# Attention's last four feature blocks are turned in mid-group, and the output projection waits for the rest only later

## What is computed

```python
x = x + 0.5 * _swiglu(_rmsnorm(x, ffn1_norm[l]), ...)
h = _rmsnorm(x, mix_norm[l])
...
x = x + jnp.concatenate([out_a, out_b, out_c], axis=-1) @ w_out[l]
x = x + 0.5 * _swiglu(_rmsnorm(x, ffn2_norm[l]), ...)
```

## Time and profile before

| | us |
|---|---|
| median of 3 runs | 3964.32 |
| lowest and highest | 3961.46 and 3968.23 |
| the profiled execution, its own time | 3960.14 |
| its span | 3958.5 |

### The profile page before, as it was taken

The page is one execution under the profiler, slowest core; times in us unless marked ns, Lnnn a source line. Parts: engine busy times, 40 slices in busy tenths (PEclk is TensorE's granted clock), DMA queues, the critical chain, the costliest instruction groups (busy, mean ns, idle before and its releaser), DMA issues. The chain is left out here.

```text
span 3958.5 us, 52357 instructions
## 1 busy us (share of the span) xinstructions
PE 3764.8 (95%) x18864; PEld 3120.0 (79%) x18864; DVE 2414.1 (61%) x4293; ACT 1457.2 (37%) x2499; POOL 132.3 (3%) x288
## 2 busy tenths in 40 slices
PE   8999989999899998999989999899999889898999
PEld 6888777888688877788868888788888658687887
DVE  6767674766667668476764355455555674645555
ACT  4223363222422245422245456322222454533322
POOL 0000030000000002100000000000000000000000
PEclk9999999999999999999999999999999999999999
DMA  6443303443544331244321110122121110003332
GB/s 240 134 137 95 104 22 122 134 137 107 188 133 138 101 101 43 88 143 131 118 78 48 59 45 21 58 65 64 58 64 58 46 36 1 27 16 97 96 95 74
DMA packets 100285, 348.72 MB, mean 88 GB/s; under 512 B 10963, under 2 KB 14547, under 8 KB 99336
## 3 DMA queue, kind: packets, MB, share of 16 engines
q1 hardware_dynamic: 73732, 264.97, 21.3%
q0 software_dynamic: 16960, 62.92, 4.9%
q10 hardware_dynamic: 9412, 18.41, 1.3%
HBM read 344.11 MB, written 12.63 MB: 90 GB/s over the span
## 5 line engine op out<-in xcount | busy, mean ns | idle before, releaser
L227 PE MATMUL ps<-h_hi,w_hi 128*128 128x512 f32 (+1 forms) x2824 | 1092.6, 387 | 78.5 <-DVE h_lo L469 34.9
L228 PE MATMUL ps<-h_lo,w_hi 128*128 128x512 f32 (+1 forms) x2824 | 1081.1, 383 | 0.0
L229 PE MATMUL ps<-h_hi,w_lo 128*128 128x512 f32 (+1 forms) x2824 | 1080.0, 382 | 0.0
L227 PEld LDWEIGHTS ps<-h_hi,w_hi 128*128 128x128 f32 x2824 | 537.3, 190 | 195.8 <-issue 41.6
L191 ACT ACTIVATE w_hi<-w_first_raw 128x1024 fp32r<-128x1024 f32 x302 | 319.4, 1059 | 972.5 <-PE ps L229 968.6
L228 PEld LDWEIGHTS ps<-h_lo,w_hi 128*128 128x128 f32 x2824 | 537.3, 190 | 103.1 <-issue 3.4
L229 PEld LDWEIGHTS ps<-h_hi,w_lo 128*128 128x128 f32 x2824 | 536.4, 190 | 103.1
L205 DVE TENSOR_TENSOR w_lo<-w_first_raw,w_hi 128x1024 fp32r<-128x1024 f32 x310 | 379.3, 1224 | 359.8 <-ACT w_hi L191 359.3
L227 PE MATMUL ps<-a_hi,w_hi 128*128 128x512 f32 x1472 | 549.9, 374 | 10.0 <-DVE x L750 6.8
L228 PE MATMUL ps<-a_lo,w_hi 128*128 128x512 f32 x1472 | 546.8, 371 | 0.0
L229 PE MATMUL ps<-a_hi,w_lo 128*128 128x512 f32 x1472 | 545.8, 371 | 0.0
(11 more groups left out here) (295 smaller groups left out, 4662.5 us busy)
## 6 DMA issues: line engine op xcount, KB each, us to landing
w_first_raw<-in_w_first SPq DMA_DIRECT2D x214, 512.0 KB, 3.6
w_raw<-in_w_first SPq DMA_DIRECT2D x104, 512.0 KB, 3.6
shared<-in_w_ada POOLq DMA_DIRECT2D x96, 512.0 KB, 4.4
w_first_raw<-in_w_mlp SPq DMA_DIRECT2D x64, 512.0 KB, 3.6
w_raw<-in_w_mlp SPq DMA_DIRECT2D x64, 512.0 KB, 3.6
bias_rows<-bias_line ACTq DMA_DIRECT2D x2, 5120.0 KB
w_first_raw<-in_w_even SPq DMA_DIRECT2D x16, 512.0 KB, 3.5
near_stage<-in_near POOLq DMA_DIRECT2D x32, 256.0 KB, 2.9
```

Source lines behind the costliest of these rows:

```text
L227: pe.matmul(out, lhs[0], rhs[0], start=start, stop=False)
L228: pe.matmul(out, lhs[0], rhs[1], start=False, stop=False)
L229: return pe.matmul(out, lhs[1], rhs[0], start=False, stop=stop)
```

## The change

Three things. The first turn step of the last group (only where a query block is two groups) moves from after the last unit to unit 8g + 4, into the other bank of the pair; its blocks 0 to 3 are the output of the group before. The projection's wait is cut in parts: in the first stack it waits at its first tile for all turn steps but the last, and for the last at its third tile; in the odd layer it waits only at the third tile; in the even layer the first tile does the 512 tokens first, after the wait for all but the last step, then waits for the last step and does the context. The wait for `out_done` goes.

```diff
@@ Project.tensor
-                o_ready(pe)
+
+                def part(g, p, q, s):
+                    n, stream = self.n0 + 4 * g + p, self.streams[s]
+                    for f in range(2):
+                        m = mm3(pe, ps[:, self.bank(g, q, s), 0:stream["n"]],
...
+                    return m
+
+                several = range(len(self.streams))
                 for g in range(2):
                     for p in range(4):
-                        n = self.n0 + 4 * g + p
-                        self.st.ready(pe, n)
+                        self.st.ready(pe, self.n0 + 4 * g + p)
+                        if g == 0 and p == 0:
+                            for s in several:
+                                o_ready(pe, p, s)
+                                for q in range(4):
+                                    m = part(g, p, q, s)
+                            m.then_inc(self.st.used, 1)
+                            continue
+                        if g == 0:
+                            o_ready(pe, p, 0)
                         for q in range(4):
                             if g == 1 and p == 0 and len(self.streams) > 1:
                                 pe.wait_ge(self.x_done, q + 1)
...
+                            for s in several:
+                                m = part(g, p, q, s)
...
@@ Attention.__init__
                         if 8 * g + 8 >= len(units):
-                            at, bank = len(units), 6 + (g + p) % 2
+                            at, bank = len(units), 6 + g % 2
+                            if len(turns[g]) == 8 and p == 0:
+                                at, bank = 8 * g + 4, 6 + (g - 1) % 2
@@ Attention.tensor, turn
-                    pe.wait_ge(self.out_done, g + 1)
+                    early = bank != 6 + g % 2
+                    pe.wait_ge(self.out_done, g if early else g + 1)
                     if k:
-                        pe.wait_ge(self.chunk_lo, k - (bank != 6 + g % 2))
+                        pe.wait_ge(self.chunk_lo, k)
@@ Attention
+            def first_turned(self, pe):
+                pe.wait_ge(self.chunk_lo, self.turn_total - 1)
@@ first_block
-                        proj.tensor(pe, lambda eng: (att.all_turned(eng),
-                                                     eng.wait_ge(att.out_done, 2 * NQ)))
+                        def turned(eng, p, s):
+                            if p == 0:
+                                att.first_turned(eng)
+                            if p == 2:
+                                att.all_turned(eng)
+                        proj.tensor(pe, turned)
@@ even_layer
-                        proj.tensor(pe, lambda eng: (att.all_turned(eng), eng.wait_ge(att.out_done, n_groups)))
+                        def turned(eng, p, s):
+                            if p == 0 and s == 0:
+                                att.first_turned(eng)
+                            if p == 0 and s == 1:
+                                att.all_turned(eng)
@@ odd_layer
-                        proj.tensor(pe, lambda eng: (atts[1].all_turned(eng), eng.wait_ge(atts[1].out_done, NQ)))
+                        def turned(eng, p, s):
+                            if p == 2:
+                                atts[1].all_turned(eng)
```

More of the change, by code:

```diff
@@ L776, in tensor @@
             def tensor(self, pe, o_ready):
-                o_ready(pe)
+                def part(g, p, q, s):
+                    n, stream = self.n0 + 4 * g + p, self.streams[s]
+                    for f in range(2):
+                        m = mm3(pe, ps[:, self.bank(g, q, s), 0:stream["n"]],
+                                self.st.at(n, f * 512 + q * 128, f * 512 + q * 128 + 128),
+                                (stream["h"][0][:, 2 * p + f, :], stream["h"][1][:, 2 * p + f, :]),
+                                p == 0 and f == 0, p == 3 and f == 1)
+                    return m
+                several = range(len(self.streams))
                 for g in range(2):
                     for p in range(4):
-                        n = self.n0 + 4 * g + p
-                        self.st.ready(pe, n)
+                        self.st.ready(pe, self.n0 + 4 * g + p)
[8 more added lines that the diff above has]
+                            o_ready(pe, p, 0)
                         for q in range(4):
```

## The result

| | before | after |
|---|---|---|
| median, runs shown with the forecast | 3964.32 (3 runs) | |
| median, all runs of the comparison | 3961.46 (5 runs) | 3942.58 (5 runs, 3941.59 to 3944.52) |
| profiled execution, its own time | 3960.14 | 3944.52 |
| its span | 3958.5 | 3942.9 |

The ratio is 0.9950 with a 95% interval of 0.9936 to 0.9965: faster by 18.9 us, between 14 and 25. The forecast was 3950.5 us, the range 3944 to 3960.

A forecast was written before the change was run, and what follows sets the result against it. TensorE, busy for 95% of the span, was taken as the bound. Waits net -8.1 us (10.0 gained, 1.9 lost) and clock -5.7 gave -13.8, from the median 3964.3 to 3950.5 us; range 3944 to 3960.

The forecast's parts named there:

- What bounds, and the waits that go: TensorE bounds; its waits before the projection shrink by 2.74 us at three ends, 1.8 in the odd layer, 10.0 in sum.
- The step that moves: The turn step moved into the attention loop delays the last values or scores: 0.7, 0.7 and 0.5 us, 1.9 lost.
- The cover named for ACT's and DVE's part of the last step: Projection tiles of about 5.4 us hide that work after the last transposes; without this cover 2.7 us would be back.
- The clock at three ends: Behind the projection starts of the first stack and even layer the clock stays full: 5.7 us gained.
- 0 for the odd layer: At the odd layer's projection start the clock falls anyway, already behind 0.84 us of idle time: no clock gain.
- -15.7 us: Alternative sum: by the skill's rule, earlier work spares the odd layer its low clock too, 1.9 us more.
- B: Rival: the clock falls anyway at the projection starts, only waits are gained: -8.1, 3956.2 us; chance 0.25.
- C: Rival: ACT and PE delays add up in the attention loop, 3.75 us instead of 1.9; 3960 us; chance 0.11 with E.
- D: Rival: low clock for 12 us behind each projection start, 24 us together against 7.8 now: +8, 3972 us; chance 0.04.
- E: Rival: the projection still waits at its start for the moved step; no size given; chance 0.11 together with C.
- Weight supply: Projection weight tiles are asked for 2 to 4 us earlier, while fetches fill the DMA engines: no cost, 10.2 us to spare.
- the even layer's order: The even layer's first tile does all 512-column matmuls ahead of the 256-column ones, the same 48: no cost.

The follow-up runs named there:

- The filled wait: Kernel before plus seven extra 512-column matmuls (four in the odd layer) ahead of the projection's wait: 3951.07 against 3956.84 us, ratio 0.9987.
- The move-only kernel: Kernel before with only the turn step moved into the last group, the projection still waiting for everything at its start: 3954.65 against 3956.84 us, ratio 0.9998.
- the second profile of before: The kernel before, unchanged, run and profiled once more: 3959.33 against 3961.25 us, ratio 0.9990.
- the second comparison: The change itself run once more, beside three further kernels, against the kernel before: 3941.24 against 3957.10 us, ratio 0.9962.
- two half measures: Kernel before with only the projection's waits split, 3948.58 us, and with only the turn step moved, 3954.65 us, each against 3956.84 us.

## Why the prediction was right or wrong

- **What bounds, and the waits that go:** right. From transposes to projection 0.41 us against the 0.5 taken (three ends), so 2.83 and not 2.74 us each. In the odd layer 2.50 us went, not 1.8: the 1.11 us for four transposes, which I kept as the price, was itself low clock. Sum 11.0 us, forecast 10.0.
- **The step that moves:** right in size and place. 0.65, 0.65 and 0.44 us, 1.7 in sum, forecast 1.9. The cover named for ACT's and DVE's part of the last step held: nobody waited.
- **The clock at three ends:** right. From the projection's start to the first split 7.26, 7.43 and 11.10 us before, 5.81, 5.79 and 8.69 after: 1.45, 1.64 and 2.41 us, 5.5 in sum, forecast 5.7. The filled wait shows that it is PE's second idle time, and not the step or the place.
- **The step that failed: "0 for the odd layer".** It gained 1.85 us of clock (7.65 to 5.80), and 0.7 us with the transposes. I read one profile's clock fall behind 0.84 us of idle time as a property of the place. The move-only kernel and the second profile of before, with the same idle times, show it elsewhere or not at all. The first profile of before had the counter-example too: at 3354.47, behind the same 0.84 us of idle time, four transposes took 0.66 us, and the clock was still full at the dense matmuls from 3356.97 on, after 1.84 us more. The Trainium skill's rule that activity releases the throttle (TensorE: Matmul & The Clock Gate, "What's actually happening"), by which I worked out -15.7 us, was nearer to the 16.6 us at the ends than the row I set against it. What the runs show is that the clock did not fall there; what releases it, none of them singles out.
- **The sum:** 11.0 - 1.7 + 5.5 + 1.85 = 16.6 us at the ends, forecast 13.8. Against the profiled execution the forecast was 3946.3 us, and 3944.5 came. The medians differ by 18.9 us, 2.3 more than the ends; the second comparison had 15.9, so these 2.3 us are not put down to the change.
- **The level, a second cause of the miss:** the forecast stood on a median of three runs, 3964.3. With five it is 3961.5, and later comparisons had 3956.8, 3957.1 and 3961.3. I had the profiled time 4.2 us under the median in hand and took the higher one. The range's low end allowed for the odd layer (1.9) or for the level, not for both, and so missed by 1.4 us. Of the 7.9 us between 3950.5 and 3942.6, 2.9 are this level, 2.8 the ends and 2.3 are not explained.
- **The rivals:** B (the clock falls anyway) did not happen at 34 starts without the second idle time. C (delays add up in the loop) did not: 1.7, not 3.75 us. D (a long stretch at low clock) was not seen at any start; its 7.8 us for the low clock of now should read 7.65, as its own 15.8 us does. E did not happen. Weight supply and the even layer's order cost nothing that shows.

## What to carry to other kernels

At a hand-over between two stages, count not only what TensorE waits but also what clock it finds afterwards: here 11 us of waiting came with 7.4 us of low clock, and two half measures gave 9.2 us where the whole gave 16.6, because each left a second idle time of 1.45 or 1.79 us, and with it much of the low clock. Before calling the clock at some place fixed, look at the other places of the same trace with the same idle times, and at a second execution of the same program; and forecast from both levels that the runs offer. Putting work that does not need the last hand-over ahead of it took a dozen lines here and hid its wait, 0.95 us at each end.

## What the runs showed that was not expected

- The same idle times (0.84 and 1.79 us) gave three outcomes in three executions: low clock from the transposes on, from the projection on, or not at all. After 0.84 and 1.45 us it fell at two of three ends of the same kernel in one execution.
- Matmuls whose result nobody reads, 1.84 us of them in a wait (1.17 us in the odd layer), made the kernel faster, 0.9987 (0.9978 to 0.9996): in the whole time hardly more than two sets of runs of one program differ by, at the four ends 7.5 us.
- Two sets of runs of one program differed by 0.1% (0.9990, 0.9981 to 0.9999), half of what I had called measurable.
